# Two blocks of a transformer stack in fp32 on one core: who divides the softmax by its sums

## What is computed

```python
s = einsum('bhqd,bhkd->bhqk', q, k) * scale        # scores
s = where(causal_or_window, s, -inf)
p = softmax(s, axis=-1)                            # differential heads: p[0] - lam * p[1]
out = einsum('bhqk,bhkd->bhqd', p, v)
```

## Time and profile before

| | |
|---|---|
| median of 3 runs | 2448.39 us (2444.46 to 2449.74) |
| the profiled execution's own time | 2446.53 us |
| its span, first to last instruction | 2444.7 us |
| TensorE products | 2282.7 us busy, 93% |
| TensorE weight loads | 1962.0 us, 80% |
| VectorE | 1547.1 us, 63%, 2855 instructions |
| ScalarE | 1060.9 us, 43%, 1884 instructions |
| GpSimd | 60.6 us, 2% |
| DMA from HBM | 392.00 MB, 161 GB/s over the span |
| mean granted TensorE clock | 0.968 of full |

### The profile page before, as it was taken

The page is one execution under the profiler, slowest core; times in us unless marked ns, Lnnn a source line. Parts: engine busy times, 40 slices in busy tenths (PEclk is TensorE's granted clock), DMA queues, the critical chain, the costliest instruction groups (busy, mean ns, idle before and its releaser), DMA issues. The chain is left out here.

```text
span 2444.7 us, 36610 instructions
## 1 busy us (share of the span) xinstructions
PE 2282.7 (93%) x13814; PEld 1962.0 (80%) x13814; DVE 1547.1 (63%) x2855; ACT 1060.9 (43%) x1884; POOL 60.6 (2%) x73
## 2 busy tenths in 40 slices
PE   5989998999989999989999999989999999989998
PEld 3646777989967677788998999757997999757997
DVE  4796607677644673466776766674766666684765
ACT  2323334555533334354555554234554544334544
POOL 0000001200000000120000000000000000000000
PEclk8999999999999999989999999989999999989999
DMA  7755232444454523334544555213553445213542
GB/s 311 277 196 192 104 138 80 171 163 180 180 206 181 207 104 112 150 111 168 195 180 155 199 187 198 78 52 144 194 190 142 178 183 199 85 52 129 206 180 94
DMA packets 37891, 394.38 MB, mean 161 GB/s; under 512 B 4480, under 2 KB 5152, under 8 KB 6048
## 3 DMA queue, kind: packets, MB, share of 16 engines
q1 hardware_dynamic: 37440, 388.87, 42.8%
q10 hardware_dynamic: 352, 4.23, 0.4%
HBM read 392.00 MB, written 1.08 MB: 161 GB/s over the span
## 5 line engine op out<-in xcount | busy, mean ns | idle before, releaser
L1368 PE MATMUL bank<-h,ring 128*128 128x256 f32 x2048 | 472.4, 386 | 5.7 <-ACT h L1128 4.1
L1368 PEld LDWEIGHTS bank<-h,ring 128*128 128x128 f32 x2048 | 386.3, 192 | 89.1 <-issue 21.9
L734 DVE TENSOR_TENSOR ffn_w_lo<-ring,ffn_w_hi 128x2048 fp32r<-128x2048 f32 x126 | 288.9, 2293 | 165.9 <-ACT ffn_w_hi L683 165.8
L604 PE MATMUL bank<-ffn_hh,ffn_w_hi 128*128 128x512 f32 x1408 | 362.1, 399 | 13.3 <-DVE ffn_hh L864 11.0
L604 PEld LDWEIGHTS bank<-ffn_hh,ffn_w_hi 128*128 128x128 f32 x1408 | 257.1, 191 | 66.1 <-issue 9.2
L656 PE MATMUL bank<-ffn_g_hi,ffn_w_hi 128*128 128x256 f32 x1056 | 299.3, 283 | 6.2 <-DVE ffn_g_lo L779 6.1
L656 PE MATMUL bank<-ffn_g_lo,ffn_w_hi 128*128 128x256 f32 x1056 | 298.8, 283 | 0.0
L656 PE MATMUL bank<-ffn_g_hi,ffn_w_lo 128*128 128x256 f32 x1056 | 298.8, 283 | 0.0
L683 ACT ACTIVATE ffn_w_hi<-ring 128x2048 fp32r<-128x2048 f32 x126 | 240.1, 1906 | 0.8
L656 PEld LDWEIGHTS bank<-ffn_g_hi,ffn_w_hi 128*128 128x128 f32 x1056 | 202.7, 192 | 7.4 <-issue 7.4
L656 PEld LDWEIGHTS bank<-ffn_g_lo,ffn_w_hi 128*128 128x128 f32 x1056 | 202.7, 192 | 0.0
(11 more groups left out here) (291 smaller groups left out, 3194.3 us busy)
## 6 DMA issues: line engine op xcount, KB each, us to landing
ring<-w_in SPq DMA_DIRECT2D x244, 1536.0 KB, 6.4
work<-cs_between ACTq DMA_DIRECT2D x2, 2048.0 KB, 8.8
x<-x_in SPq DMA_DIRECT2D x1, 1024.0 KB, 15.1
mem<-mem_in SPq DMA_DIRECT2D x1, 1024.0 KB, 7.0
y_out<-x SPq DMA_DIRECT2D x4, 256.0 KB, 2.6
con<-con_in SPq DMA_DIRECT2D x1, 801.0 KB, 7.0
par<-par_in SPq DMA_DIRECT2D x2, 302.0 KB, 15.5
work<-pos_in SPq DMA_DIRECT2D x2, 128.0 KB, 6.1
```

The costliest lines, as they stand in the source:

```text
L604: pe.matmul(up_out(j, half, False), w_hi[:, j % 2, c0:c0 + P], hh[:, k, :, :], start=k == 0, stop=False)
L734: dve.tensor_tensor(w_lo[:, j % 2, UP], ring[:, (base + j) % RING, UP], w_hi[:, j % 2, UP], ALU.subtract).then_inc(S(tag + "_up_lo"), 1)
L1368: m = pe.matmul(ps[0:m_rows, 0:T], tile(t0 + k, base)[:, 0:m_rows], rhs, start=k == 0, stop=k == len(src) - 1)
```

## The change

The two scalings of a unit on VectorE go, for units 8 to 15 of `mixer1` and for all units of `mixer2`. VectorE's prob step ends with the reciprocal, which signals `rc_ready`. ScalarE gets a prob step: it waits for `rc_ready`, makes two 128 by 128 diagonals out of the identity, one for each half of the queries (a copy with the reciprocal as its scale), and signals `prob_ready`. In the turn TensorE multiplies each block of the raw exponentials by the diagonal of its half rather than transposing it by the identity, so that the transposed block comes out scaled. There are two buffers of diagonals, and the two waits that guard them. Units 0 to 7 of `mixer1` stay as they are.

```diff
+            diag = cut(512, (2, 2, P))
...
                         for b_ in range(3):
-                            m = pe.transpose(bank[5][:, b_ * P:b_ * P + P], probs[:, j % 3, b_ * P:b_ * P + P],
-                                             C("ident", P))
+                            part = probs[:, j % 3, b_ * P:b_ * P + P]
+                            if j >= 8:
+                                m = pe.matmul(bank[5][:, b_ * P:b_ * P + P], part, diag[:, j % 2, min(b_, 1), :], start=True,
+                                              stop=True)
+                            else:
+                                m = pe.transpose(bank[5][:, b_ * P:b_ * P + P], part, C("ident", P))
                         m.then_inc(S("tp_ready"), 1)
...
+                    elif step == "prob" and j >= 8:
+                        act.wait_ge(S("rc_ready"), j - 7)
+                        if j >= 10:
+                            act.wait_ge(S("tp_ready"), turned(head_of(j - 2)) + 1)
+                        for c in range(2):
+                            ins = act.activation(diag[:, j % 2, c, :], C("ident", P), ACT.Copy, scale=rc[:, j % 2, c:c + 1])
+                        ins.then_inc(S("prob_ready"), 1)
...
                         dve.wait_ge(S("exp_done"), j + 1)
+                        if j >= 8:
+                            if j >= 10:
+                                dve.wait_ge(S("prob_ready"), head_of(j - 2) + 1)
+                            dve.reciprocal(rc[:, j % 2, :], sm[:, j % 2, :]).then_inc(S("rc_ready"), 1)
+                            continue
                         v.link(dve.reciprocal(rc[:, j % 2, :], sm[:, j % 2, :]))
-                        if head_of(j) is None or j >= 8:
+                        if head_of(j) is None:
                             for c, cols in enumerate((slice(0, 128), slice(128, 384))):
                                 ins = dve.tensor_scalar(pb[:, cols], pb[:, cols], rc[:, j % 2, c:c + 1], None, ALU.mult)
-                                if head_of(j) is None:
-                                    v.link(ins)
-                            if head_of(j) is not None:
-                                ins.then_inc(S("prob_ready"), 1)
+                                v.link(ins)
...
+                            second = parts_of(j)[1][0]
                             for a_, b_ in moves:
-                                m = pe.transpose(bank[5][:, b_:b_ + P], probs[:, j % 3, a_:a_ + P], C("ident", P))
+                                m = pe.matmul(bank[5][:, b_:b_ + P], probs[:, j % 3, a_:a_ + P],
+                                              diag[:, j % 2, int(a_ >= second), :], start=True, stop=True)
...
+                        elif step == "prob":
+                            act.wait_ge(S("rc_ready"), j + 1)
+                            if j >= 2:
+                                act.wait_ge(S("tp_ready"), tseq["turn", "", j - 2] + 1)
+                            for c in range(2):
+                                ins = act.activation(diag[:, j % 2, c, :], C("ident", P), ACT.Copy,
+                                                     scale=rc[:, j % 2, c:c + 1])
+                            ins.then_inc(S("prob_ready"), 1)
...
-                            v.link(dve.reciprocal(rc[:, j % 2, :], sm[:, j % 2, :]))
-                            for c, (c0, c1) in enumerate(parts_of(j)):
-                                pb = probs[:, j % 3, c0:c1]
-                                ins = dve.tensor_scalar(pb, pb, rc[:, j % 2, c:c + 1], None, ALU.mult)
-                            ins.then_inc(S("prob_ready"), 1)
+                            if j >= 2:
+                                dve.wait_ge(S("prob_ready"), j - 1)
+                            dve.reciprocal(rc[:, j % 2, :], sm[:, j % 2, :]).then_inc(S("rc_ready"), 1)
```

## The result

| | before | after |
|---|---|---|
| median | 2449.06 us of 4 runs (2444.46 to 2449.98) | 2471.69 us of 4 runs (2469.97 to 2475.0) |
| ratio, 95% interval | | 1.0095 [1.0083, 1.0107] |
| the profiled execution's own time | 2446.53 us | 2469.97 us |
| its span | 2444.7 us | 2468.4 us |
| mean granted TensorE clock | 0.968 | 0.967 |

The change costs 23.3 us (20.3 to 26.2 by the interval), and 23.7 by the two spans. It was predicted slower, but by 10.5 us: 2471.69 is above the range that the prediction gave, 2451 to 2468.

What follows compares the result with a forecast made beforehand. It took TensorE, busy 93% of the span, as the bound. Waits of 3.20 us per `mixer1` and 2.03 per `mixer2`, two layers each, gave 10.5 us more: a median of 2458.9 us, range 2451 to 2468.

Steps and rivals of the forecast that it cites:

- I count nothing: In the changed turns, swapping transposes for ordinary fp32 products (48 in `mixer1`, 68 in `mixer2`) adds no time, both 273 ns.
- the fourth rival: In the changed turns, an ordinary product costs four transposes: 38 us more, 2497 us; chance 0.02.
- Turns 8, 12 and 15: `mixer1`: TensorE waits for diagonals queued behind exponentials (8, 12: +0.96 us each) or the copy of values (15: +1.15).
- Turn 10: `mixer1`: the diagonals delay ScalarE's squares and the copies behind them, and TensorE waits for the last copy: +0.13 us.
- `mixer2`, turn 2: Diagonals push ScalarE's root and so VectorE by 0.60 us, and diagonals 2 come 0.87 late: together +1.47 us.
- Ahead of turn 5: `mixer2`: diagonals 5 stand ahead of ScalarE's copy of V, for which TensorE waits: +0.56 us.
- The first rival: TensorE's longer idle ahead of `mixer1` turn 8, or `mixer2`, brings half clock: 3 to 9 us more, 2462 to 2468; chance 0.17.
- The queue part: All waits from the diagonals' place in ScalarE's queue, in both mixers: 10.5 us.
- The second rival: VectorE bounds the second half of `mixer2`, gaining 3.8 us a layer: 2447 us, no change; chance 0.09.
- The third: In `mixer2`, the clock doesn't fall at 1636: up to 4 us a layer back, 2451 us; chance 0.08.

Runs made afterwards that it cites:

- diagonals only: Changed kernel, but the turn transposes by the identity and the probs' scaling is left out; ScalarE's diagonals are waited for but unused: 2462.61 us, ratio 1.0047.
- one pass everywhere: Changed kernel with exponentials and diagonals written as fp32r in both mixers' changed units, so each product is one record: 2462.77 us, ratio 1.0050.
- last diagonals early: "diagonals only" with the diagonals of unit 15 of `mixer1` moved ahead of ScalarE's copy of the values of unit 13: 2459.65 us, ratio 1.0047.
- one pass in `mixer2`: Changed kernel with probs and diagonals written as fp32r in `mixer2` only, so the product there is one record: 2468.23 us, ratio 1.0087.
- by GpSimd: Changed kernel, but GpSimd rather than ScalarE makes the diagonals: 2470.15 us, ratio 1.0091.
- one pass, by GpSimd: Changed kernel with fp32r exponentials and diagonals, so products are one record, and GpSimd making the diagonals: 2453.77 us, ratio 1.0012.
- before, two passes: Kernel before, with prob ahead of soft in only pass 13 of `mixer1` and pass 3 of `mixer2`: 2452.8 us, ratio 1.0016.

## Why the prediction was wrong

**The step that failed** is the prediction's "I count nothing", for the product: a term put at nothing that is 13.1 us. It compared 273 ns with 273 ns, the lengths of one record, and never asked how many records a product has. The same rows had the answer: 24 turns of three blocks show x72, one a block, while the 24 heads' products with the second part of V show x48, two each. With 0.11 us between neighbours of one line, which the fourth rival used, the term is 116 x 0.113 = 13.1 us, and the run with the product alone measures 15.9 (12.7 to 18.9). 10.5 + 13.1 = 23.6 against 23.3 measured, but that so near a fit is luck in part: some 2 us of the 13.1 fall into waits (0.34 at turn 12, 0.68 ahead of turn 2 of a `mixer2`, two layers each), `mixer2` is less late than forecast, and 4.8 us of the trace's lag come from half clock outside the turns, of which no run shows how much belongs to the change.

**The fourth rival** had the right mechanism with the wrong factor: twice, not four times, and 13 us, not 38. It got a chance of 0.02 because rows 2 and 3 were read as speaking against it. The rule of the Trainium skill (Perfetto Trace Analysis, Transposes) that a logical transpose should not be a standard product was right here, and the run with only the product gives its price, 15.9 us in this kernel. The "4× faster for FP32" of the Trainium skill (TensorE: Matmul & The Clock Gate, Terms) is two times in these traces: one record for two.

**Turns 8, 12 and 15**, forecast +0.96, +0.96 and +1.15: measured +0.95, +0.95 (0.62 in after, where the product of turn 11 fills the rest) and +1.12. The cost of a diagonal (0.39) and of a pair (0.69, measured 0.68) held. Turn 10, forecast +0.13, shows nothing.

**`mixer2`, turn 2**, forecast +1.47: measured 0.83. The step took it that the diagonals push the root by 0.60 and so VectorE. It left out that VectorE runs without a gap into soft 2, so that its own missing scaling brings the exponentials, and the root, 0.6 sooner. What remains is the diagonals' own, 0.87 by the forecast. Ahead of turn 5, +0.56: measured 0.53, a wait of 2.03 for the 2.1 named. In "diagonals only" some 0.8 a layer of these two comes back in the stretches of half clock. The one behind turn 5 keeps its place there (1636 to 1649 before, 1648 to 1661, 12 us on as the stage is), while TensorE comes to it later by the two waits; that this is why less work is done at half clock is argued from the lag and not tested. The runs without the second record add 0.4 to 0.7 a layer, for 2.03.

**The first rival** (clock falls behind turn 8) happened in one of two layers of after's profiled execution, in both of "diagonals only" and of "one pass everywhere", and in neither of "last diagonals early", which has the same waits there. The queue part alone measures 11.5 and 12.3 us where 10.5 was forecast, although `mixer2` adds only a third of its share. So the sum is right by luck in part: in the two profiled executions where the clock falls this makes up for the rest. In "last diagonals early" 8.2 was due by the forecast and 11.5 measured without a fall behind turn 8; where its time goes stays open.

**The second rival** (VectorE bounds `mixer2`, which gains 3.8 us a layer) didn't occur: with both costs taken away a `mixer2` changes by 0.1 and 0.2 us, and the time is still 2.9 us above before. **The third** (the clock doesn't fall at 1636) occurred in part: in after it falls there still, but comes back after some 7 us and not 13, and 3.7 and 3.5 us are given back.

The parts, measured alone, are 15.9 and 11.5, together 27.4 with about 4.5 of uncertainty, against 23.3 for both. Their sum need not be exact: the wait ahead of turn 2 of a `mixer2` takes in the longer products of turns 0 and 1, and the half-clock stretches lie differently in each.

## What to carry to other kernels

Before one operation replaces another on the same engine, count records per call and not only the length of one: in this kernel an fp32 product is two records, a transpose one, and the length of a record says nothing of it. When work goes from one in-order queue to another, follow the queue it enters and also what the queue it leaves will now start sooner. Here an exchange in an order that all engines share moved waits rather than removed them, so look one pass further on before it is counted as a gain.

## What the runs showed that was not expected

- The fall of the clock behind turn 8 is not settled by the wait ahead of it. After 2.74 or 2.75 us the profiled execution of after keeps full clock in one layer and falls in the other, "diagonals only" falls in both, "last diagonals early" and "one pass in `mixer2`" in neither. After 2.58 us "by GpSimd" falls in neither layer and "one pass, by GpSimd" in one. After 1.80 us, the wait of the kernel before, "before, two passes" falls in one.
- Runs of one kernel differ with the mean granted clock: the kernel before took 2443.0 us of span at 0.971 and 2449.0 to 2452.3 at 0.966, up to 0.4%. An effect of 2 us can be read in the trace and not in the time.
- GpSimd takes 0.60 us for a 128 by 128 scaling by a column in `mixer1`, 0.60 to 1.07 in `mixer2`; ScalarE 0.39 in both.
